# A two-layer decoder trunk on one core: three of the second quad's down matrices get room of their own, and the small routing loads change their queue

## What is computed

```python
for layer in range(DEPTH):
    hn = rms_norm(h, norm_mix[layer])
    mix = nsa_stickbreak_mixer(hn, ...) if layer % 2 == 0 else hgrn2_mixer(hn, ...)
    h = h + mix
    h = h + hier_moe(rms_norm(h, norm_ffn[layer]), moe_w_grp[layer], ...)
return rms_norm(h, final_norm)

# hier_moe: group, then two experts in the group; combine = their weights
hid = silu(einsum('sd,edf->sef', xs, w_gate)) * einsum('sd,edf->sef', xs, w_up)
return einsum('sef,efd->sd', hid * combine[..., None], w_down)
```

## Time and profile before

| | us |
|---|---|
| median of 3 runs (lowest, highest) | 797.61 (797.05, 799.07) |
| the profiled execution, its own time | 800.14 |
| its span, first to last instruction | 798.3 |

### The profile page before, as it was taken

The page is one execution under the profiler, slowest core; times in us unless marked ns, Lnnn a source line. Parts: engine busy times, 40 slices in busy tenths (PEclk is TensorE's granted clock), DMA queues, the critical chain, the costliest instruction groups (busy, mean ns, idle before and its releaser), DMA issues.

```text
span 798.3 us, 11774 instructions
## 1 busy us (share of the span) xinstructions
PE 646.0 (81%) x4874; PEld 447.5 (56%) x4874; DVE 319.7 (40%) x495; ACT 219.9 (28%) x475; POOL 152.5 (19%) x103
## 2 busy tenths in 40 slices
PE   7978897797996955865969989998899965865865
PEld 7976786597443413313259989997765413313412
DVE  5446465616222202202278999453342302202204
ACT  4424444432120100100144553553311100100102
POOL 6024330340000000000043488352200000000000
PEclk9987999999998987978989999998999987977989
DMA  9992235376799999999995535439759999999993
GB/s 295 272 379 77 106 107 220 121 293 238 309 420 420 422 422 420 422 422 421 405 364 192 203 114 196 148 106 392 276 219 425 418 422 423 420 422 422 420 417 142
DMA packets 62191, 246.07 MB, mean 308 GB/s; under 512 B 4400, under 2 KB 12800, under 8 KB 40640
## 3 DMA queue, kind: packets, MB, share of 16 engines
q1 hardware_dynamic: 60608, 242.33, 77.3%
q0 software_dynamic: 864, 2.39, 0.9%
q10 hardware_dynamic: 672, 0.68, 0.3%
HBM read 244.34 MB, written 1.05 MB: 307 GB/s over the span
## 4 chain that ended last, share of the span: by engine, by line
PE 46%; DMA 29%; DVE 12%; ACT 4%; SPq 4%; issue 3%; POOL 2%; ACTq 0%; DVEq 0%
DMA ring<-in_moe_w_down 24%; PE psum L1989 7%; PE psum L1616 7%; PE psum L1936 6%; PE psum L1618 4%; PE psum L1625 4%; DMA ring<-in_moe_w_up 3%; PE psum L1620 2%; PE psum L1929 2%; PE psum L1920 2%; PE psum L1627 2%; SPq L417 2%; DVE arena L1476 2%; POOL w_lo L344 2%; DMA ring<-in_att_w_in 2%
## 5 line engine op out<-in xcount | busy, mean ns | idle before, releaser
L344 POOL TENSOR_TENSOR w_lo<-ring,w_hi 128x1024 fp32r<-128x1024 f32 x44 | 109.8, 2510 | 163.7 <-ACT w_hi L712 163.7
L1936 PE MATMUL psum<-arena,xT 128*32 128x512 f32 x512 | 69.7, 706 | 49.7 <-DMA arena<-in_moe_w_up 49.7
L1390 DVE TENSOR_TENSOR arena<-psum,arena 128x256 f32<-128x256 f32 x16 | 6.8, 425 | 235.8 <-ACT arena L911 235.8
L1936 PE MATMUL psum<-ring,xT 128*32 128x512 f32 x512 | 65.4, 669 | 34.6 <-DMA ring<-in_moe_w_up 34.6
L712 ACT ACTIVATE w_hi<-ring 128x1024 fp32r<-128x1024 f32 x64 | 65.0, 1051 | 80.2 <-PE psum L1625 43.3
L1936 PEld LDWEIGHTS psum<-arena,xT 128*32 128x32 f32 x512 | 17.5, 127 | 97.2 <-DMA arena<-in_moe_w_up 50.8
L1616 PE MATMUL psum<-x_hi,w_hi 128*128 128x256 f32 x256 | 66.5, 295 | 3.0 <-DVE q_lo L1109 1.3
L907 ACT ACTIVATE arena<-psum 128x256 f32<-128x256 f32 x16 | 6.1, 383 | 223.2 <-PE psum L1936 223.2
L1989 PE MATMUL psum<-ring,arena 128*32 128x512 f32 x512 | 58.2, 595 | 8.0 <-DMA ring<-in_moe_w_down 6.8
L1929 PE MATMUL psum<-arena,xg 128*128 128x128 f32 x512 | 60.3, 275 | 0.7 <-DVE arena L1377 0.7
L1920 PE MATMUL psum<-xT,arena 128*128 128x512 f32 x128 | 57.9, 595 | 2.9 <-DVE xT L1396 2.9
(11 more groups left out here) (298 smaller groups left out, 1096.1 us busy)
## 6 DMA issues: line engine op xcount, KB each, us to landing
ring<-in_moe_w_down SPq DMA_DIRECT2D x64, 1024.0 KB, 20.7
ring<-in_moe_w_gate SPq DMA_DIRECT2D x32, 1024.0 KB, 20.6
ring<-in_moe_w_up SPq DMA_DIRECT2D x32, 1024.0 KB, 22.1
arena<-in_moe_w_gate SPq DMA_DIRECT2D x32, 1024.0 KB, 25.9
arena<-in_moe_w_up SPq DMA_DIRECT2D x32, 1024.0 KB, 26.4
ring<-in_rec_w_in SPq DMA_DIRECT2D x16, 1024.0 KB, 14.6
ring<-in_att_w_in SPq DMA_DIRECT2D x8, 1024.0 KB, 11.5
ring<-in_att_w_out SPq DMA_DIRECT2D x4, 1024.0 KB, 9.4
```

The lines of the kernel that those rows point to most:

```text
L344: eng.tensor_tensor(quarter_lo(base, r), quarter(base, r), quarter_hi(r).bitcast(F32), ALU.subtract)\
L1936: return pe.matmul(bank(3)[e * CAP:(e + 1) * CAP, :].rearrange("p (w f) -> p w f", w=2), gatheredT[:, k, e * CAP:(e + 1) * CAP], w, start= ...
```

## The change

It makes 24 KB of room per partition and puts three of the four down matrices of the second quad (quad 1) of each expert stage there:

- `dynamic_dma_scratch_size=1024` leaves GpSimd's DMA scratch 1 KB of 16 KB. Two small buffers become parts of others (`iota_i`, `lb_rows`). The new buffer `ahead` holds 16 KB, the down matrices of experts 0 and 1 of quad 1.
- The two halves of expert 2's matrix go to `square_moe` (4 KB, where the norm's squares were) and `gain` (4 KB, the norm gain), once the norm ahead of the experts has used them.
- Expert 3's matrix still goes to the ring, after down product 0.
- SP issues these three loads right behind quad 0's down matrices (`load_ahead`).
- The gains of the next norm (`gain_load(2)` and `gain_load(4)`) wait for down product 1.
- The routing matrices and biases leave GpSimd's queue for ACT's. Layer 0's are issued after the first `xT_half`, layer 1's and `lb_rows` after the SiLU of quad 0 in the first expert stage.
- TensorE's loop over quads starts at quad 4; quads 2 and 3 are written out, since the counts that down product 1 waits for differ.

```diff
-        arena_t = sb("arena", [P, 19600])
+        ahead = sb("ahead", [P, UW])
+        arena_t = sb("arena", [P, 19584])
...
+        def down_part(l, n, e, j):
+
+            if n == 1 and e < 2:
+                return ahead[:, (e * KF + j) * D:(e * KF + j + 1) * D]
+            if n == 1 and e == 2:
+                return square_moe if j else gain[:, :]
+            return down_slots(l, n == NQ - 1)[e // 2].rearrange("p (e j n) -> p e j n", e=2, j=KF)[:, e % 2, j, :]
...
+        def load_ahead(sp, l):
+
+            v = 2 * l + 1
+            for e in range(2):
+                sp.dma_start(ahead[:, e * KF * D:(e + 1) * KF * D],
+                             second_down(l)[e].rearrange("p j n -> p (j n)")).then_inc(s["ahead_loaded"], 16)
+            sp.wait_ge(s["norm_rstd"], TT * v + TT)
+            sp.dma_start(down_part(l, 1, 2, 1), second_down(l)[2][:, 1, :]).then_inc(s["ahead_loaded"], 16)
+            sp.wait_ge(s["xg_done"], TT * v + TT)
+            sp.dma_start(down_part(l, 1, 2, 0), second_down(l)[2][:, 0, :]).then_inc(s["ahead_loaded"], 16)
...
                 load_down(sp, l, 0)
+                load_ahead(sp, l)
...
                 sp.wait_ge(s[f"down{l}"], 1)
-                load_down(sp, l, 1)
+                sp.dma_start(down_slots(l)[1][:, KF * D:2 * KF * D],
+                             second_down(l)[QE - 1].rearrange("p j n -> p (j n)")).then_inc(s[f"down_loaded{l}"], 16)
...
-                if v:
-
+                if v % 2:
                     pool.wait_ge(s["xg_done"], TT * v)
+                else:
+                    pool.wait_ge(s[f"down{v // 2 - 1}"], 2)
                 pool.dma_start(gain[:, :], src.partition_broadcast(P)).then_inc(s["gain_loaded"], 16)
...
-            route_load(0)
             gain_load(1)
...
-            route_load(1)
+
...
+            def route_load(l):
+                act.dma_start(w_route[:, :, 0:GR], moe_w_grp[l].rearrange("(p k) n -> p k n", k=KD))\
+                    .then_inc(s["route_loaded"], 16)
+                act.dma_start(w_route[:, :, GR:GR + NE], moe_w_exp[l].rearrange("(p k) n -> p k n", k=KD))\
+                    .then_inc(s["route_loaded"], 16)
...
-            act.dma_start(lb_rows[0:2 * RH, :], rec_lb_logits.rearrange("l (h p) -> (l h) p", p=RK))\
-                .then_inc(s["rec_small"], 16)
...
             for t in range(TT):
                 xT_half(0, t)
+            route_load(0)
...
                 silu(l, 0)
+                if l == 0:
+                    act.wait_ge(s["route_used"], 1)
+                    route_load(1)
+                    act.dma_start(lb_rows[0:2 * RH, :], rec_lb_logits.rearrange("l (h p) -> (l h) p", p=RK))\
+                        .then_inc(s["rec_small"], 16)
...
-                down(l, 0)
+                down(l, 0, early=True)
...
-                with pe.Fori(1, NQ // 2) as i:
+                body(l, 2, 0, early=True)
+                body(l, 3, 1)
+                with pe.Fori(2, NQ // 2) as i:
...
-    nc = bacc.Bacc("TRN2", target_bir_lowering=False, num_devices=1)
+    nc = bacc.Bacc("TRN2", target_bir_lowering=False, num_devices=1, dynamic_dma_scratch_size=1024)
```

More of the change, by code:

```diff
@@ L184, in hybrid_trunk @@
         rank = sb("rank", [P, NE])
-        iota_i = sb("iota_i", [P, NE], I32)
         norm_sum = sb("norm_sum", [P, 2 * NL + 1, TT])
@@ L195, in hybrid_trunk @@
         route_s = sb("route_s", [P, 16, TT])
+        iota_i = route_t[:, 0, 0, :].bitcast(I32)
         chosen = sb("chosen", [P, 2, TT, NE])
+        lb_rows = chosen[:, :, :, :].rearrange("p a t e -> p (a t e)")
         member = sb("member", [P, TT, NE])
@@ L202, in hybrid_trunk @@
         passes = [sb(f"passes{l}", [1, 1], I32) for l in range(NL)]
-        lb_rows = sb("lb_rows", [P, P])[:, :]
         gnorm = sb("gnorm", [P, RV])[:, :]
-        arena_t = sb("arena", [P, 19600])
+        ahead = sb("ahead", [P, UW])
+        arena_t = sb("arena", [P, 19584])
         psum = ctx.enter_context(nc.psum_tensor("psum", [P, 8, 512], F32))
@@ L427, in load_down, with second_down @@
                     .then_inc(s[f"down_loaded{l}"], 16)
+        def second_down(l):
+            return moe_w_down[l].rearrange("(q e) (p j) n -> q e p j n", e=QE, p=P)[1]
+        def load_ahead(sp, l):
[7 more added lines that the diff above has]
+            sp.dma_start(down_part(l, 1, 2, 0), second_down(l)[2][:, 0, :]).then_inc(s["ahead_loaded"], 16)
         def load_last_down(sp, l):
@@ L597, in _ @@
                                     pattern=[[1, P]], channel_multiplier=-1))
-            link(pool.iota(iota_i[:, :], pattern=[[1, NE]], base=0, channel_multiplier=0))
-            link(pool.tensor_copy(rank[:, :], iota_i[:, :]))
+            link(pool.iota(iota_i, pattern=[[1, NE]], base=0, channel_multiplier=0))
+            link(pool.tensor_copy(rank[:, :], iota_i))
             link(pool.tensor_scalar(iota_slot[:, :], rank[:, 0:CAP], 1.0, None, ALU.add))
@@ L748, in xT_half @@
                     .then_inc(s["xT_front"], 1)
+            def route_load(l):
[3 more added lines that the diff above has]
+                    .then_inc(s["route_loaded"], 16)
+                act.dma_start(b_route[0:GR, :], moe_b_grp[l].rearrange("(n one) -> n one", one=1))\
+                    .then_inc(s["route_loaded"], 16)
+                act.dma_start(b_route[GR:GR + NE, :], moe_b_exp[l].rearrange("(n one) -> n one", one=1))\
+                    .then_inc(s["route_loaded"], 16)
             act.preload_act_table_set("natural_log_exp_and_others")
@@ L1972, in turn_hidden, with down @@
                 last.then_inc(s[f"hid_psum{l}"], 1)
-            def down(l, n, last_quad=False, later_round=False):
+            def down(l, n, last_quad=False, later_round=False, early=False):
                 pe.wait_ge(s[f"hidT{l}"], n + 1)
@@ L1978, in down @@
                     pe.wait_ge(s["last_down_front"], 32 * (l + 1))
+                elif early:
+                    pe.wait_ge(s[f"down_loaded{l}"], 64 + 16 * n)
+                    if n:
+                        pe.wait_ge(s["ahead_loaded"], 64 * (l + 1))
                 elif later_round:
-                    pe.wait_ge(s[f"down_loaded{l}"], 64 * n)
+                    pe.wait_ge(s[f"down_loaded{l}"], 64 * n - 48)
                 else:
-                    pe.wait_ge(s[f"down_loaded{l}"], 64 * (n + 1))
-                w = [v.rearrange("p (e j n) -> p e j n", e=2, j=KF) for v in down_slots(l, last_quad)]
+                    pe.wait_ge(s[f"down_loaded{l}"], 64 * n + 16)
+                kind = n if early else NQ - 1 if last_quad else 2
                 for j in range(KF):
@@ L1990, in down, with body @@
                                              hidT[:, j, e * CAP:(e + 1) * CAP],
-                                             w[e // 2][:, e % 2, j, c * 512:(c + 1) * 512],
+                                             down_part(l, kind, e, j)[:, c * 512:(c + 1) * 512],
                                              start=(j == 0), stop=(j == KF - 1))
                 last.then_inc(s[f"down{l}"], 1)
-            def body(l, n, parity):
+            def body(l, n, parity, early=False):
                 pe.wait_ge(s[f"added{l}"], 4 * n - 4)
@@ L2001, in body @@
                 later_gate_up(l, n, parity)
-                down(l, n - 1)
+                down(l, n - 1, early=early)
                 pe.wait_ge(s[f"shareT{l}"], n)
```

## The result

The changed kernel is a little slower than the one before: a median of 803.92 us (800.54 to 808.59, 20 runs) against 799.47 us (797.05 to 804.86, 20 runs). The ratio is 1.0045, with a 95% interval from 1.0028 to 1.0062, so +3.6 us (2.2 to 5.0); the medians themselves lie 4.4 us apart. The profiled execution has a span of 801.5 us, against 798.3 before.

The account below looks back on a forecast made before the run. Expert stages are bound by their weight bytes at 422 GB/s once the stream starts. Start +5.5, first stage +9, second -6.2 sum to +8.3 us: 808.4 profiled, less 2.5 for the median, forecast 806 us, range 786 to 810.

Parts of the forecast that it names:

- the likeliest case: Both routing-load places: ACT held by its own full DMA queue, +8.3 us in sum, range 800.5 to 810; chance 0.46.
- Terms 1 and 2: Each expert stage: three matrices loaded ahead save 7.5 us, gain loads moved into the full stream cost 1.2 us.
- margins of 3 and 5 us: Expert stage: time to spare before quad 3's gate/up loads and the next down matrices, so the shortened stream stays unbroken.
- The start: First weight split: ACT, held by layer 0's routing loads, resumes near 20 instead of 14.2; +5.5 us (2.5 to 7).
- The first stage: First expert stage: ACT's hold opens a 13.7 us hole in the stream; -6.2+13.7+1.5 = +9 us (5 to 11).
- turn by turn draining: DMA engines: each small piece of ACT's waits for one of SP's pieces; an 8 KB piece takes 0.31 us.
- The two adders: First expert stage: gate/up product of 6.87 us behind the late down product; 1.5 us for TensorE slowed after idling.
- The signature that I named: ACT's issue of the 128 B rows takes 5 us near 14 and some 14 us near 210, if held.
- the 80 that I had read from SP's queue: DMA queues: an issuing engine is held at about 80 outstanding pieces per DMA engine.
- Not held at all: Rival, ACT's routing loads: pieces travel together or ACT's queue is deeper; -10.2 us, 787.4 (785 to 792); chance 0.38.
- Half held: Rival, ACT's routing loads: 16 B pieces travel in twos; total -0.5 us, 797 (793 to 801); chance 0.16.
- The loads ahead gain nothing: Rival, expert stages: loads reach past 204.5 or SP's queue holds them; 821 or 802; no chance of its own.

Follow-up runs that it names:

- Experiment 1: Changed kernel with layer 0's routing loads issued by SP instead of ACT, layer 1's still on ACT: 797.53 us, ratio to the kernel before 0.9964.
- experiment 2: Changed kernel with layer 1's routing loads issued by SP instead of ACT, layer 0's still on ACT: 790.53 us, ratio to the kernel before 0.9882.
- experiment 7: Kernel before, nothing loaded ahead, with the routing loads on ACT at the changed kernel's two places: 813.06 us, ratio 1.0155.
- experiment 8: Changed kernel with only the two routing matrices on ACT, biases and small table moved to SP: 787.34 us, ratio to the kernel before 0.9823.
- experiment 9: Changed kernel with ACT issuing the small loads ahead of the two routing matrices, same places: 786.95 us, ratio to the kernel before 0.9831.
- experiment 5: Changed kernel with only the group matrix moved from ACT to SP, for both layers: 787.06 us, ratio to the kernel before 0.9822.
- experiment 3: Changed kernel with both layers' routing loads on SP instead of ACT: 783.83 us, ratio to the kernel before 0.9788; run again 784.82 us, 0.9801.
- experiment 4: Kernel before with both layers' routing loads on SP instead of GpSimd, nothing loaded ahead: 800.90 us, ratio 1.0007.

## Why the prediction was right or wrong

**The direction and the mechanism** were right: ACT is held by its own queue in both places, as the likeliest case had it, and the changed kernel is slower. The measured time of 803.92 lies in that case's own range (800.5 to 810). The size was too large: +8.3 forecast, +3.6 (2.2 to 5.0) measured. The number came out closer than the change: 806 stands on the 797.61 of three runs, and the median of the kernel before over 20 runs is 799.47. By spans (+3.2) the missing 5.1 us are in the main 1.5 at the start, 1.6 in the first stage and 2.1 between the stages.

**Terms 1 and 2** together were -6.2 us a stage. Stage 2 gives -6.1 in the changed kernel; without the hold stage 1 gives -6.2. Their margins of 3 and 5 us held: with both loads on SP the stream has no gap in these windows.

**The start** was +5.5. The split came 5.3 us late, and at the opening of stage 1 4.0 us were left. Experiment 1 gave 6.4 us by medians, and the stage opened at 178.4 to 183.3 in the profiles of all kernels without the hold and at 186.6 to 187.2 in the three with it. "Kept to the end" is right within that scatter. That 5.3 came so near to 5.5 is in part luck. ACT's queue moved nothing before 16.0, 3.6 us behind the first issue where I had 2, and when ACT was let go it had moved 443 packets, 28 per engine, not 50 (18 in experiments 2 and 7).

**The first stage** was +9 and measured +7.4, of which 1.6 are the clock's, so +5.8. This is the term that was mis-sized most: I had ACT free 18.2 us behind the SiLU's last step, and it was 15.3. The turn by turn draining was right, but only 35 pieces per engine had to go, not 50 (see Pieces). The two adders were right on the whole: the down product, not the gate/up product, ran slow (4.97 for 3.57), as the idle clock suggested, and the gate/up product took 6.87 as before. I had charged 1.5 us for it; 1.4 were paid.

**The step that failed** is which issue is held. I wrote that the second matrix fits only once 50 pieces have drained "and ACT does nothing meanwhile". In fact the second issue took 0.8 us, and the third was held (experiments 8 and 9). For the sum it made no difference, since small loads stood behind in both places; for a cure it makes all of it. The signature that I named, 5 and 14 us on the issue of the 128 B rows, appeared as 5.24 and 12.48 us on the bias behind it.

**Pieces.** The rule of one packet per row held to the last packet. ACT's queue shows now

```profile
q10 hardware_dynamic: 4944, 0.98, 0.7%
```

Those are its packets in the whole span, 4272 more than the 672 of the earlier trace rows. Two layers give 2 x (65+65) x 16 = 4160, and the biases 2 x (4+4+32+16) = 112. The Trainium skill's "DMA: Bandwidth & Descriptors" (Queues, rings and completion order) calls 9 to 17 descriptors typical of a packet; on this queue the profile has one packet for every row, so the rival that rested on pieces travelling together fell.

That the engines take turns piece by piece can be read from the changed kernel's queues from 220 to 228 us, and the number of pieces that ACT waits for from 216.52 to 229.03, the time of its held issue (q1 is SP's queue, q10 ACT's; packets, MB, share of 16 engines):

```profile
q1 hardware_dynamic: 444, 3.24, 96.9%
q10 hardware_dynamic: 444, 0.01, 3.2%
...
q10 hardware_dynamic: 559, 0.01, 2.6%
```

One of SP's for one of ACT's, 0.29 us for such a pair on an engine. ACT was let go when 559 packets, 35 per engine, had gone and some 95 of the 130 were left (93 and 97 in experiments 1 and 7; 102 to 112 at the start). So the 80 that I had read from SP's queue was too low a count for this one; what sets the number is open.

**The rivals.** *Not held at all* describes what the change would have been with its issues in another order: experiments 5, 8 and 9 came to 787.06, 787.34 and 786.95 for its 787.4. As changes they are -14.2, -14.2 and -13.5 us, more than its -10.2; the times agree because the kernel before took 800.2 and 800.6 beside them, not 797.61. *Half held* fell: packets of 16 B rows did not travel in twos (its terms add up to -0.7, not -0.5). *The loads ahead gain nothing* fell as I had meant it, since experiment 3 gains 6.2 us in each stage; in the changed kernel's first stage they do gain next to nothing, but through the hold.

**Not forecast:** the 2.1 us between the stages, which experiment 4 leaves to the scatter; its cause was not looked for. Neither was the clock's 1.6 us. And SP's two extra waits were not over by 184: the norm's last use of `gain` ended at 187.5 in the kernel before, and the load into `gain` went out at 191.54 in the changed one. It cost nothing, as the next load came at 209.06.

## What to carry to other kernels

Before a load is moved from one DMA queue to another, count its pieces per DMA engine (rows over 16, not bytes): 144 KB of routing weights in 16 B and 128 B rows cost ACT 5 and 12 us, where a load of 1 MiB in 8 KB rows costs SP 0.4 while its queue has room. An engine that computes should issue the load with many rows last, or leave it to a queue on which nobody waits. And where loading ahead thins out the stream behind it, a stall at that place can get dearer: a hold of 12 to 13 us cost 7.4 us without the room and 12 to 14 with it. Compare stages between several executions before naming a cause for a us or two: here TensorE's clock alone moved a stage by 1.6 us.

## What the runs showed of the hardware

- A load of 130 pieces per engine in two issues did not hold ACT (0.64 and 0.77 us, 0.55 and 0.81 us); a third issue behind it was held for 4.4 to 5.2 us at the start, where SP's packets were of some 1.4 KB on the mean (1.42 MB in 1027 packets), and for 12.0 to 13.2 us beside pieces of 8 KB. I had expected the second to be held.
- While both queues had work, the engines moved one packet of each in turn: 444 and 444 in 8 us of the changed kernel, 452 and 452 in experiment 9 (218 to 226). ACT was let go with 93 to 112 of its 130 pieces per engine left.
- With the small loads first, the last issue took 1.62 us in the stage (0.76 at the start; 7 pieces stood ahead of the 130), so there may be some hold left even there.
- In experiment 5 ACT's issues took at most 0.89 us (at 13.67 us), inside an issue of SP that was held for 5.14 us (from 10.99): a held SP did not hold ACT.
- GpSimd's queue moved the same four loads of a layer in 144 packets, ACT's in 2136.
